# The experts' inner values spread over the column groups by inner column, and turned in 32x32 blocks on VectorE

## The reference, cut to what matters

```python
def moe_ffn(u, w_router, b_router, w_gate, w_up, w_down):
    logits = (u @ w_router).astype(F32) + b_router.astype(F32)
    probs = jax.nn.softmax(logits, axis=-1)
    top_p, top_i = lax.top_k(probs, TOP_K)
    top_p = top_p / jnp.sum(top_p, -1, keepdims=True)
    gates = jnp.sum(jax.nn.one_hot(top_i, N_EXPERTS, dtype=F32) * top_p[..., None], axis=-2)
    y = jnp.zeros(u.shape, F32)
    for e in range(N_EXPERTS):
        h = jax.nn.silu(u @ w_gate[e]) * (u @ w_up[e])
        y = y + gates[..., e:e + 1] * (h @ w_down[e]).astype(F32)
    return y.astype(u.dtype)
```

## Time and profile before

| | us |
|---|---|
| median of three executions | 1149.36 |
| lowest, highest | 1147.52, 1150.23 |
| span of the profiled execution, first to last instruction | 1142.5 |
| steps 3 to 69 of the experts and what stands between them, within it | 748.7 to 1121.8 |
| PE busy | 1093.2 (96%) |
| DVE busy | 724.2 (63%) |
| ACT busy | 568.6 (50%) |
| DMA, mean over the span | 242 GB/s |

### The profile page before, as it was taken

The page is one execution under the profiler, slowest core; times in us unless marked ns, Lnnn a source line. Parts: engine busy times, 40 slices in busy tenths (PEclk is TensorE's granted clock), DMA queues, the critical chain, the costliest instruction groups (busy, mean ns, idle before and its releaser), DMA issues. The chain is left out here.

```text
span 1142.5 us, 26917 instructions
## 1 busy us (share of the span) xinstructions
PE 1093.2 (96%) x10785; PEld 753.1 (66%) x10785; DVE 724.2 (63%) x1543; ACT 568.6 (50%) x1038; POOL 164.6 (14%) x244
## 2 busy tenths in 40 slices
PE   6998999899999999999999999999999999999996
PEld 3566789779999999777679887633333356333533
DVE  1576855875444445577865778766756756657667
ACT  2252332436434333245323324568778777677463
POOL 8000004000000000000003100122233323223130
PEclk9999999999999999999999999999999999999998
DMA  9848493496545455724485355499999999999871
GB/s 309 300 141 285 171 315 138 179 327 207 176 152 181 132 173 175 228 79 181 148 250 183 118 187 206 162 359 368 386 356 370 352 317 370 385 333 347 310 281 42
DMA packets 172916, 276.46 MB, mean 242 GB/s; under 512 B 7894, under 2 KB 105200, under 8 KB 167673
## 3 DMA queue, kind: packets, MB, share of 16 engines
q1 hardware_dynamic: 160768, 264.01, 66.3%
q10 hardware_dynamic: 12024, 10.73, 3.3%
HBM read 268.42 MB, written 6.30 MB: 240 GB/s over the span
## 5 line engine op out<-in xcount | busy, mean ns | idle before, releaser
L2095 ACT COPY CP<-XW 128x512 f32 (+1 forms) x490 | 253.4, 593 | 100.5 <-PE bank L1669 75.1
L2891 DVE COPY CP<-XW 128x512 f32 (+1 forms) x490 | 209.6, 472 | 123.2 <-PE bank L1669 93.1
L1669 PE MATMUL bank<-CP,UG 128*32 128x512 f32 (+1 forms) x1536 | 164.0, 557 | 0.0
L1036 POOL COPY CP<-XW 128x512 f32 (+1 forms) x140 | 110.3, 795 | 372.2 <-PE bank L1669 286.6
L2260 DVE TENSOR_TENSOR lo<-raw,hi 128x2048 fp32r<-128x2048 f32 (+1 forms) x42 | 95.8, 2281 | 86.0 <-ACT hi L2041 48.6
L1669 PEld LDWEIGHTS bank<-CP,UG 128*32 128x32 f32 x1536 | 59.3, 110 | 85.8 <-issue 64.8
L1048 PE MATMUL bank<-UH,hi 128*128 128x288 f32 x352 | 104.7, 297 | 2.1 <-DVE UL L2248 1.9
L1223 PE MATMUL bank<-UM,raw 128*128 128x288 f32 x416 | 105.9, 409 | 0.0
L1021 POOL TENSOR_TENSOR SD<-SD,EG 128x512 f32<-128x512 f32 x16 | 24.2, 1548 | 563.5 <-PE bank L1402 563.5
L1049 PE MATMUL bank<-UH,lo 128*128 128x288 f32 x352 | 103.8, 295 | 0.0
L1050 PE MATMUL bank<-UL,hi 128*128 128x288 f32 x352 | 103.5, 294 | 0.0
(11 more groups left out here) (495 smaller groups left out, 2011.2 us busy)
## 6 DMA issues: line engine op xcount, KB each, us to landing
raw<-in_w_ada_dram SPq DMA_DIRECT2D x48, 1024.0 KB, 6.9
XW<-in_w_exp_down_dram SPq DMA_DIRECT2D x44, 1024.0 KB, 7.8
XW<-in_w_exp_gate_dram SPq DMA_DIRECT2D x32, 1024.0 KB, 9.1
XW<-in_w_exp_up_dram SPq DMA_DIRECT2D x32, 1024.0 KB, 9.1
raw<-in_w_in_dram SPq DMA_DIRECT2D x28, 1024.0 KB, 8.2
XW<-in_w_exp_gate_dram SPq DMA_DIRECT2D x16, 768.0 KB, 6.8
XW<-in_w_exp_up_dram SPq DMA_DIRECT2D x16, 768.0 KB, 7.7
raw<-in_w_ff_gate_dram SPq DMA_DIRECT2D x11, 1024.0 KB, 5.7
```

The costliest lines, as they stand in the source:

```text
L1036: pool.tensor_copy(weights(s_, NE + j).unsqueeze(1), XW[:, s_ % RING, bass.ds(unit[j], 1), 0:width(s_)]).then_inc(S("pool_copied"), 1)
L1669: mm = pe.matmul(to, x_[:, k_, UNIT * u:UNIT * u + UNIT], w_, start=(k_ == 0), stop=(k_ == LASTK[kind]))
L2095: act.copy(weights(s_, NE + j).unsqueeze(1), XW[:, s_ % RING, bass.ds(unit[j], 1), 0:width(s_)]).then_inc(S("act_copied"), 1)
L2891: dve.tensor_copy(weights(s_, NE + j).unsqueeze(1), XW[:, s_ % RING, bass.ds(unit[j], 1), 0:width(s_)]).then_inc(S("dve_copied"), 1)
```

## The change

**Gate and up.** A unit no longer belongs to one column group. Its weights' columns are dealt out over the four groups in runs of 32: group `q` takes columns 128j + 32q to 128j + 32q + 31 of every 128 (`split_columns`). So a unit is four matmuls of 128 columns (96 in the narrow block) with the same stationary tile, one for each group, and a set of four units is 16 matmuls in place of four of 512 (384). Their outputs stand side by side in the bank, unit `x` of the set at column 128x (96x). Only the first unit of a bank starts the accumulation. Set 6 is four matmuls in each block; in the narrow one of 96 columns, where three of 128 stood.

**Turning.** PSUM partition 32q + i now has slot i of every unit, and in the columns the inner columns of group `q`. A transposition within 32x32 blocks puts inner column 128j + 32q + i on partition 32q + i, which is what down wants. `turn_h` and its copies on ACT are gone. DVE does it from `SGX` to `HX`, one `dve.transpose` of 128x512 (128x384) for a set and a small one for set 6, at places from the table `TURN`: for blocks 0 and 1 one in each of the six steps from one step after the block, behind set 3, and set 6's in the last of these behind set 5; for block 2 two in each of steps 49 to 51 and one in 52. `HX` is flat, a unit's blocks behind each other (`h_of`).

**Waits.** ACT's silu of blocks 1 and 2 waits until the block before is turned (`SGX` is written again). The `rest` tasks move from steps 51 and 52 to 54 and 55, since `ZO` lies over `SGX`; ACT's copy waits for all 21 turns.

```diff
-for _c in range(len(WIDTH)):
-    for _t, _at in enumerate(((1, 0), (1, 2), (1, 4), (1, 6), (2, 1), (2, 3), (2, 5))):
-        AT7[2 * KT * (_c + 1) + _at[0], _at[1]] = ('turn', _c, _t)
 for _x in range(6):
-    AT7[DOWN0 + 3 + _x // 3, 2 * (_x % 3)] = ('rest', _x % 3, _x // 3)
+    AT7[DOWN0 + 6 + _x // 3, 2 * (_x % 3)] = ('rest', _x % 3, _x // 3)
...
+TURN = {(2 * KT * (_c + 1) + 1 + _t, 3): (_c, _t) for _c in range(2) for _t in range(SETS - 1)}
+TURN |= {(2 * KT * (_c + 1) + SETS - 1, 5): (_c, SETS - 1) for _c in range(2)}
+TURN |= {(DOWN0 + 1 + _t // 2, 2 + 3 * (_t % 2)): (2, _t) for _t in range(SETS)}
...
+        def split_columns(s, u):
+            return weights(s, u).rearrange("p (j q i) -> p q j i", q=PER, i=UNIT)
+        def h_of(c, u, n=1):
+            first = c * (PER * (SETS - 1) + 1) * WIDTH[0] // PER + u * WIDTH[c] // PER
+            return HX[:, first:first + n * WIDTH[c] // PER]
...
+                        else:
+                            n_ = width(s_) // PER
+                            for x, u in enumerate(units):
+                                w_ = split_columns(s_, u)
+                                for q in range(PER):
+                                    mm = pe.matmul(bank[t][UNIT * q:UNIT * q + UNIT, n_ * x:n_ * x + n_],
+                                                   UG[:, k_, UNIT * u:UNIT * u + UNIT], w_[:, q, :, :],
+                                                   start=(k_ == 0 and x == 0), stop=(k_ == LASTK[kind] and u == units[-1]))
...
-                        for f in range(n_f):
-                            mm = pe.transpose(bank[7][:, f * P:f * P + P], SGX[:, t, f * P:f * P + P], ident[:, :])
...
+                                if c > 0:
+                                    act.wait_ge(S("h_turned"), SETS * (c - 1) + t + 1)
...
-                                act.copy(HX[:, 4 * x:4 * x + n_f, y * P:y * P + n_],
-                                         bank[7][:, 0:n_f * n_].rearrange("p (f w) -> p f w", f=n_f)).then_inc(read[7], 1)
...
                             elif what == 'rest':
                                 read7(AT7[s_, t])
+                                act.wait_ge(S("h_turned"), SETS * len(WIDTH))
...
+                            if (s_, t) in TURN:
+                                x, y = TURN[s_, t]
+                                dve.wait_ge(S("up_read"), SETS * x + y + 1)
+                                if y < SETS - 1:
+                                    dve.transpose(h_of(x, PER * y, PER), SGX[:, y, 0:WIDTH[x]]).then_inc(S("h_turned"), 1)
```

More of the change, by code:

```diff
@@ L730, in program @@
         OH = at_m("OH", 2 * NTT * D, [TT, NTT, NSLOT + P - UNIT], F32R)
-        HX = at_m("HX", 0, [P, XT, NSLOT])
+        HX = at_m("HX", 0, [P, XT * NSLOT])
         o = max(XT * NSLOT, 2 * NTT * D + NTT * (NSLOT + P - UNIT))
@@ L1660, in unit_set @@
                         set_waits(s_, t)
[L1661 to L1669, removed]
+                        units = range(PER * t, PER * t + PER if t < SETS - 1 else PER * t + 1)
+                        if kind == 'down':
+                            for q in range(PER):
+                                if t < SETS - 1:
+                                    u = PER * t + q
+                                    to, w_ = bank[t][UNIT * q:UNIT * q + UNIT, :], weights(s_, u)
+                                else:
+                                    u = PER * t
+                                    to, w_ = bank[t][UNIT * q:UNIT * q + UNIT, 0:P], weights(s_, u)[:, q * P:q * P + P]
+                                h_ = h_of(k_ // 4, u)[:, k_ % 4 * UNIT:k_ % 4 * UNIT + UNIT]
+                                mm = pe.matmul(to, h_, w_, start=(k_ == 0), stop=(k_ == LASTK[kind]))
+                        else:
+                            n_ = width(s_) // PER
+                            for x, u in enumerate(units):
+                                w_ = split_columns(s_, u)
+                                for q in range(PER):
+                                    mm = pe.matmul(bank[t][UNIT * q:UNIT * q + UNIT, n_ * x:n_ * x + n_],
+                                                   UG[:, k_, UNIT * u:UNIT * u + UNIT], w_[:, q, :, :],
+                                                   start=(k_ == 0 and x == 0), stop=(k_ == LASTK[kind] and u == units[-1]))
                         mm.then_inc(S("x_set"), 1)
@@ L1729, in step @@
                                     ug_read(pe, KT + UG_BANK.index(7))
-                                if AT7[s_, t] == ('turn', 0, 0):
+                                if AT7[s_, t] == ('rest', 0, 0):
                                     pe.wait_ge(S("share_read"), SETS)
@@ L1733, in step @@
                                     mm = mask(*of)
-                                elif what == 'turn':
-                                    mm = turn_h(*of)
                                 elif what == 'rest':
@@ L2154, in step @@
                                          bank[7][:, 0:NTT * (TT + 6)].rearrange("p (c w) -> p c w", c=NTT)[:, :, 0:TT]).then_inc(read[7], 1)
[L2155 to L2159, removed]
-                                act.copy(HX[:, 4 * x:4 * x + n_f, y * P:y * P + n_],
-                                         bank[7][:, 0:n_f * n_].rearrange("p (f w) -> p f w", f=n_f)).then_inc(read[7], 1)
-                                act.wait_ge(read[7], base[7] + IN7.index(AT7[s_, t]) + 1)
-                                act.nop().then_inc(S("h_turned"), 1)
                             elif what == 'rest':
                                 read7(AT7[s_, t])
+                                act.wait_ge(S("h_turned"), SETS * len(WIDTH))
                                 x, h = of
@@ L2930, in step @@
                                 v, src = (SGX[:, t, 0:w_], bank[t][:, 0:w_]) if t < SETS - 1 else \
-                                    (SGU[0:w_ // PER, :], bank[t][0:w_ // PER, 0:P])
+                                    (SGU[:, 0:w_ // PER], bank[t][:, 0:w_ // PER])
                                 dve.tensor_tensor(v, v, src, ALU.mult).then_inc(S("up_read"), 1)
@@ L2952, in step @@
                                     copy(s_ + 1, j)
+                            if (s_, t) in TURN:
[3 more added lines that the diff above has]
+                                    dve.transpose(h_of(x, PER * y, PER), SGX[:, y, 0:WIDTH[x]]).then_inc(S("h_turned"), 1)
+                                else:
+                                    dve.transpose(h_of(x, PER * y), SGU[:, 0:WIDTH[x] // PER]).then_inc(S("h_turned"), 1)
                             if (s_, t) not in AT7:
```

2 lines of the change are left out of this document (1 added, 1 removed).

## The result

The changed kernel takes **1282.28 us** (1276.77 to 1288.54, four runs) where the kernel before took 1148.44 in the runs beside it: a ratio of 1.118, interval 1.114 to 1.121. The forecast was 1139.1 with a range up to 1157. The prediction is wrong by 143 us, outside its range and of the other sign. The profile after is of the longest of the four executions (1288.54 us, a span of 1286.8). In this and in each later run the profiled execution lies 1.7 to 1.8 us above its span, so the profile of the kernel before, with a span of 1142.5, is of an execution of some 1144.2 us, 5 under the 1149.36 of the table, and the 6.9 us "around the instructions" are 1.7.

The account below looks back on a forecast made before the run. It took the array to bind, the weight stream just behind: -17.8 (turning removed) + 2.9 + 0.6 (array) + 4 (stream) = -10.3 us, from 1149.4 to 1139.1 us; 8-in-10 range 1135 to 1157.

Parts of the forecast that it names:

- What bounds the kernel: Gate and up steps: the array sets the step, 5.368 us wide and 4.088 narrow, with the weight stream just behind.
- Removed, 17.8 us: Turning through the array disappears from three stretches of steps: 5.13 + 5.16 + 7.55 us saved.
- The array pays 2.9 + 0.6: Smaller gate and up matmuls lengthen 32 wide steps by 0.090 us each and 16 narrow ones by 0.037.
- floor of 25 ns: Rival: no two matmul records start under 25 ns apart; narrow step 5.0 us, total 1149 us, chance 0.08.
- bound by the weight loads: Rival: in the narrow block weight loads hold each record to 27.3 ns; narrow step 5.46 us, total 1156, chance 0.12.
- lower end of this term, -0.6: Narrow steps: lowest value of the array's added cost, at 20.0 ns a record; the upper end was +21.9 us.
- The instructions are traffic too: Gate and up steps: 144 more records of 133 B, 19 KB a step on the weight stream, cost +0.05 us.
- VectorE pays nothing: Large transpositions of 0.6 us each fit into about 2.0 us free per step (1.0 in the narrow block).
- The stream takes back 4 us: Gate and up steps: weights arrive hardly faster than the steps need them, losing 4 us, between 0 and 6.
- The 6.9 us around the span: Time outside the profiled span of 1142.5 us, taken as unchanged, making 1132.2 into 1139.1 us.
- The rivals: Weight loads 0.12, start floor 0.08, stream throughout 0.12 (1145), 128 B weight runs 0.05 (1163), transpositions over cover 0.03 (1150 up).
- What would show it: Profile signs: wide steps 5.46 us, narrow 4.1 to 4.3; wrong if narrow exceeds 5.0 or steps wait beyond weights.

Follow-up runs that it names:

- e1: Changed kernel with sets 0 to 5 back on their old matmuls, VectorE still doing all the turning: 1131.83 us, ratio 0.985 to the kernel before.
- e5: Kernel before with one of the six full sets (2), and the seventh, spread and turned on VectorE: 1141.17 us, ratio 0.9956.
- e6: Kernel before with two of the six full sets (1 and 4), and the seventh, spread and turned on VectorE: 1151.16 us, ratio 1.0029.
- e8: Changed kernel with expert loads from step 3 on bringing only 16 of each 128 weight rows, an eighth of the bytes and descriptors: 1189.43 us.
- e4: Changed kernel with 256 (192) moving columns in each gate and up matmul instead of 128 (96), as many matmuls: 1370.87 us.
- e10: Kernel before with each gate and up matmul of the six full sets cut in two by columns, in place: 1156.20 us, ratio 1.0083.
- e7: Kernel before with three of the six full sets (0, 2, 4), and the seventh, spread and turned on VectorE: 1192.88 us, ratio 1.0423.
- e9: Kernel before with each gate and up matmul of the six full sets cut into four by columns, in place: 1287.17 us.

## Why the prediction was wrong, by its steps

- **What bounds the kernel** (the array, with the stream just behind): right for the kernel before, and the order of reading was sound. It did not ask what else PE lives on.
- **Removed, 17.8 us**: right, as far as it can be told from what the stream takes back; e1 has both at once and gained 16.9 by medians. By parts, from the stages of the traces: behind block 0 5.2 (5.13 predicted); behind block 1, with the narrow steps, 3.7 in e1 (5.16); in the down stage 7.7 in the changed kernel (7.55), but only 3.4 in e1. Where e1 falls short, narrow steps of up to 5.0 us, and 23.3 us in which ACT and DVE wait for weights in the down stage (5.3 before), show the stream's hand.
- **The array pays 2.9 + 0.6**: the rates are right within a burst. In e5 and e6 each spread set adds 0.015 us to a wide step, and 106 narrow records start within some 2.2 us in e8's timeline (973.72, 2.42 with the last one's own quarter microsecond), 21 ns apart against 20.6. No floor of 25 ns and no bound by the weight loads shows, so both of those rivals fall. (The lower end of this term, -0.6, is a slip: 16 steps of 25 x 8 x 20.0 ns in place of 4.088 us are -1.4. Nothing hangs on it.) **The step that failed is the one before the multiplication**: the price was read off the tail's scatter, a burst of some hundred records between sparser work, less than one piece, and the array's 64 small matmuls, and taken for a pace that holds through 9600 records. A burst shows what PE can take, not what it can be given. In place of 5.46 and 4.13 us the steps took 8.00 to 8.19, and the gate and up stages 398 us where they had taken 253.
- **"The instructions are traffic too", +0.05 us a step**: here the right quantity was counted, 133 B a record and 144 more a step, and priced wrongly, as bytes on the stream. Their bytes are 0.7% of the DMA time. What they cost is the time until each next piece is there, 4.0 us without and 5.3 to 6.5 with the stream. In the prediction's own form: 200 records / 128 = 1.56 pieces a step, times 5.3, is 8.3 us; measured 8.00, 8.18 and 8.19. A row to warn of it did stand in the profile: 87 packets over 1142 us, and its densest steps, the narrow ones, asked for one every 9.7 us.
- **VectorE pays nothing**: right, as far as e1 can show it. The large transpositions took 0.70 us (0.6 taken, within the cover of 2.0), the small ones 0.30. The trace of after, lines 2959 and 2961, ns at least, median and most:

```profile
L2959 DVE STREAM_TRANSPOSE HX<-SGX x18: 561/703/705, 883.6 to 1154.7; 128x512 f32<-128x512 f32 x12, 128x384 f32<-128x384 f32 x6
L2961 DVE STREAM_TRANSPOSE HX<-SGU x3: 272/295/298, 928.3 to 1157.0; 128x128 f32<-128x128 f32 x2, 128x96 f32<-128x96 f32 x1
```

- **The stream takes back 4 us**: e1 is where it can be read; by the medians it took 1, by the two profiles' spans 5, and the first compares more executions. In the changed kernel, with a thinned stream, it took nothing in the down stage.
- **The 6.9 us around the span**: mis-sized, since they are 1.7 and the rest is that the profiled execution was a short one. The sum starts from the median, so this does not move it.
- **The rivals**: all had the array or an operand as the bound. None named the supply, and the chances given to slower, 0.20, were spread over causes that all proved empty.
- **"What would show it"** did its work: a narrow step over 5.0 us was named as the sign of error; it read 8.2.

The 145 us in the gate and up steps are not all pauses. PE's waits for issue there are 102 us, and the bursts are longer than e8's, because the clock fell. Stretches of the changed kernel behind the pause that ended at 803.34:

```profile
804.50:807.90 3.40, 3.40 (x75) 3.40 (x68) 0.76 (x2) 1.14 (x2) 0.00 (x0) 0.51 0.89 263
808.00:811.00 3.00, 3.00 (x118) 3.00 (x113) 2.38 (x6) 2.70 (x5) 1.74 (x2) 1.00 1.00 382
```

75 records in 3.4 us at the lower level of 1.2 GHz, 118 in 3.0 at 2.4. By an estimate from the granted clock of the four stretches of gate and up steps above (0.96, 0.92, 0.90 and 0.89 over 112, 64, 120 and 80 us), some 61 us were run at the lower level, which costs up to 30 us. e4 and e8, with no pauses or with some of at most 1.5 us, kept 1.00 in these stages; e10 kept it with one of 2.4 us. e7 has 0.98 in its narrow block, where one pause lasted 2.6 us, and e9, with pauses as long as the changed kernel's, 0.92. That the long pauses bring the clock down fits every run, but no run changed the one without the other.

The Trainium skill, "Runtime: NRT & Kernel Launch", "Instruction fetch mechanics", has the blocks of 16 KB, of 256 instructions; the traces agree, with 126 to 127 records, each a matmul and a load, in a burst of one piece. It also says that fetching is mostly hidden behind the pace of issue. By that rule the changed kernel would have run as forecast; it holds here up to about one piece in 6.6 us, and fails beyond.

## What to carry to other kernels

Before cutting matmuls into smaller ones, count TensorE's instructions: fp32 takes two matmuls and two loads for each written, 128 such pairs are a piece of 16 KB, and a piece came every 4.0 us with quiet DMA queues and every 6.5 us with 320 GB/s of weights beside it (e7). Under the full stream one in 6.6 us was had without pauses (e6, e10) and one in 5.4 was not, so as an estimate from this kernel records should average no less than about 50 ns apart. In a profile the sign is "issue" ahead of matmuls at intervals of 126 or 253 records with every engine and the stream slack at once; the quick test is to cut the matmuls of the old kernel in place and change nothing else. And a price taken from a short burst needs a second look at what must be refilled when it goes on.

## What was not expected of the hardware

- A piece of instructions was ready for PE 2.2 to 2.7 us after its packet started under the stream (changed kernel, e7) and 2.2 to 3.1 under hardly any (e8's narrow block), though the packet itself took about 1 us; and in long dense work PE seldom went further than two pieces without a stop (bursts of 126 or 253, twice 379 records).
- The traffic of another queue goes with a later start of the packet: 1.1 to 2.1 us after PE went on in e8 at 37 to 44 GB/s, with the same instructions 1.1 to 4.4 in the changed kernel at 222 to 265.
- fp32 matmuls of 96 columns on the four column groups in turn started 21 ns apart in a burst (e8), each with its weight load.
- VectorE's transposition in 32x32 blocks moves 128x512 fp32 in 0.70 us.
